# One layer of a conv / matrix-memory hybrid on eight cores: squares taken from the read-out itself, chunk steps and one merge projection in another order

## What is computed

```
proj = h @ w_in + b_in            # x, b, c (1024 each), q, k (512), v, o (1024), gates, gate_c, gate_m (1024)
y_conv = bg * causal_dwconv(cg * xin, conv_mix_w)
# matrix memory, per head (4 heads, dk 128, dv 256), in chunks of 128 rows
num = wts @ v + s_inter * (q @ C_prev);  den = rowsum(wts) + s_inter * (q @ n_prev)
h   = num / max(|den|, exp(-m_t))
C   = s_old * C + k_weighted^T @ v
hm  = sigmoid(o) * rmsnorm_per_head(h, g)      # h * rsqrt(mean(h*h) + EPS)
z   = sigmoid(gate_c) * (y_conv @ w_proj_conv) + sigmoid(gate_m) * (hm @ w_proj_mlstm)
x  += gt1 * (z @ w_out);  then a gated conv FFN, residual, final norm
```

## Time and profile before

| | us |
|---|---|
| median of 3 runs (1358.87 to 1362.21) | 1359.05 |
| the profiled execution, its own time | 1363.88 |
| its span, slowest core (core 2) | 1362.6 |
| spans of the eight cores | 1348.5 to 1362.6 |
| TensorE busy / VectorE / ScalarE | 1248.0 / 687.1 / 546.8 |
| mean granted TensorE clock, core 2 | 0.979 |

### The profile page before, as it was taken

How to read it: one execution, slowest core, us unless ns; L and a number is a source line. 1 busy time by engine, 2 the same in 40 slices (tenths; PEclk the granted TensorE clock), 3 DMA queues, 4 the chain that set the end, 5 groups by cost and what they waited for, 6 DMA issues and landing times.

```text
span 1362.6 us, 21331 instructions; the slowest of 8 cores (1348.5 to 1362.6 us)
## 1 busy us (share of the span) xinstructions
PE 1248.0 (92%) x7525; PEld 689.9 (51%) x7662; DVE 687.1 (50%) x1251; ACT 546.8 (40%) x1081; POOL 76.4 (6%) x149
## 2 busy tenths in 40 slices
PE   0588999998879999999989999988999999999997
PEld 0345455566656655666644444444544444444443
DVE  0473342586723356565654413467823365556534
ACT  2465113766522235554433331555521145544202
POOL 1000000000100000000000000000000000000000
PEclk9788999999989999999999999999999999999999
DMA  9968125388692465334264674313347074431603
GB/s 175 228 186 131 25 39 83 48 123 132 95 197 44 81 128 120 63 63 78 40 132 79 178 133 80 73 32 62 80 107 119 15 145 93 82 74 32 108 1 124
DMA packets 35128, 130.38 MB, mean 96 GB/s; under 512 B 2764, under 2 KB 3020, under 8 KB 35024
## 3 DMA queue, kind: packets, MB, share of 16 engines
q0 software_dynamic: 24944, 93.74, 41.1%
q1 hardware_dynamic: 10080, 35.27, 8.0%
HBM read 214.34 MB, written 8.39 MB: 163 GB/s over the span
## 4 chain that ended last, share of the span: by engine, by line
PE 83%; DMA 5%; DVE 5%; issue 3%; ACT 3%; POOL 0%; DVEq 0%; SPq 0%; ACTq 0%; POOLq 0%
PE psum L509 54%; PE psum L1270 11%; PE psum L805 4%; PE psum L1125 4%; DMA wslot<-w_in 3%; PE psum L1366 2%; PE psum L714 2%; PE psum L485 2%; DMA arena<-xin 1%; DMA arena<-bada_row 1%; PE psum L878 1%; ACT xnb L914 1%; DVE C L880 1%; ACT sqj L434 1%; ACT arena L871 1%
## 5 line engine op out<-in xcount | busy, mean ns | idle before, releaser
L509 PE MATMUL psum<-arena,wslot 128*128 128x512 bf16 (+1 forms) x4542 | 823.1, 338 | 17.1 <-DVE arena L926 9.0
L509 PEld LDWEIGHTS psum<-arena,wslot 128*128 128x128 bf16 x4640 | 452.6, 98 | 362.1 <-issue 24.0
L1199 DVE SCALAR_TENSOR_TENSOR arena<-arena,pcol_t 128x1028 f32<-128x1028 f32 (+1 forms) x88 | 113.2, 1287 | 92.8 <-ACT arena L1196 88.2
L1270 PE MATMUL psum<-wslot,arena 128*128 128x512 bf16 x688 | 151.8, 379 | 2.6 <-ACT arena L489 1.5
L1081 ACT ACTIVATE arena<-psum,pcol_t 128x512 bf16<-128x512 f32 (+1 forms) x80 | 47.9, 603 | 163.2 <-PE psum L509 162.2
L1270 PEld LDWEIGHTS psum<-wslot,arena 128*128 128x128 bf16 x704 | 68.9, 98 | 84.0 <-issue 2.0
L434 ACT ACTIVATE sqj<-arena 128x1024 bf16<-128x1024 f32 (+1 forms) x49 | 51.7, 1055 | 143.1 <-DVE arena L1273 97.4
L1201 ACT ACTIVATE arena<-arena 128x1028 f32<-128x1028 f32 (+1 forms) x44 | 46.6, 1059 | 121.1 <-DVE arena L1199 121.0
L1085 DVE TENSOR_TENSOR arena<-psum,arena 128x512 f32<-128x512 f32 (+1 forms) x40 | 23.4, 586 | 74.7 <-PE psum L509 73.8
L1125 PE MATMUL psum<-wslot,arena 128*128 128x512 bf16 (+1 forms) x264 | 59.2, 379 | 0.8 <-ACT arena L489 0.4
L805 PE MATMUL psum<-wslot,arena 128*128 128x512 bf16 (+1 forms) x266 | 58.9, 379 | 0.4 <-issue 0.2
(11 more groups left out here) (176 smaller groups left out, 1065.5 us busy)
## 6 DMA issues: line engine op xcount, KB each, us to landing
wslot<-w_in POOLq DMA_DIRECT2D x32, 1024.0 KB, 12.3
arena<-xin SPq DMA_DIRECT2D x32, 512.0 KB, 14.9
wslot<-w_ada POOLq DMA_DIRECT2D x12, 1024.0 KB, 15.5
wslot<-w_up_a POOLq DMA_DIRECT2D x10, 1024.0 KB, 9.8
wslot<-w_up_g POOLq DMA_DIRECT2D x10, 1024.0 KB, 12.2
wslot<-w_down POOLq DMA_DIRECT2D x8, 1024.0 KB, 8.6
y<-arena SPq DMA_DIRECT2D x16, 512.0 KB, 2.7
xt<-xin SPq DMA_DIRECT2D x15, 512.0 KB, 5.7
```

The source lines that it names most:

```text
L509: S.op("pe", lambda e: e.matmul(psum[:, b, 0:n], lhsT=wv[:, k, wcol0:wcol0 + 128], rhs=src[:, k, t0:t0 + n], start=(k == 0), stop=(k == 7) ...
L1199: S.op("dve", lambda e: e.scalar_tensor_tensor(out=t3[:, T0:NT], in0=a_s[:, s_ + T0:s_ + NT], scalar=pcol[:, cw + s_:cw + s_ + 1], in1=t3[ ...
L1270: S.op("pe", lambda e: e.matmul(psum[:, b, :], lhsT=act_t[jj][:, t0:t0 + 128], rhs=wv[:, jj % 8, :], start=(jj == 0), stop=(jj == NFF - 1) ...
```

## The change

1. `at_sq` squares `Xs` as it is, no longer scaled by `d4`, so it no longer waits for `at_den`. `at_den` ends with `d4*d4` in place of the reciprocal. A new step `at_rms` adds `256*EPS*d4^2` to the sum of squares on VectorE and takes the root on ScalarE. `at_f` is one reciprocal, its multiply is gone. (num/den/sqrt(mean((num/den)^2)+EPS) is num/sqrt(mean(num^2)+EPS*den^2).)
2. The table `parts` has other positions.
3. In the merge the memory projection of column block 0 is issued behind gate_c and conv of column block 1, and gate_m of block 1 behind it; from block 2 on the order is as before. No load moves on SP's queue; POOL issues the same weight loads in the same order.

```diff
-                S.op("dve", lambda e: e.reciprocal(out=d4[j][0:p], in_=d4[j][0:p]), reads=[r_d4[j]], writes=[r_d4[j]])
+                S.op("dve", lambda e: e.tensor_tensor(out=d4[j][0:p], in0=d4[j][0:p], in1=d4[j][0:p], op=ALU.mult), ...)
...
-                                                       scale=d4[j][0:p, h:h + 1], accum_out=s4[j][0:p, h:h + 1]),
-                         reads=[r_Xs[0], r_d4[j]], writes=[r_sqj, r_s4[j]])
-                if 3 in hh:
-                    S.op("act", lambda e: e.activation(out=s4[j][0:p], in_=s4[j][0:p], func=AF.Sqrt, scale=1.0 / 256, bias=EPS), ...)
+                                                       accum_out=s4[j][0:p, h:h + 1]),
+                         reads=[r_Xs[0]], writes=[r_sqj, r_s4[j]])
+            def at_rms(c):
+                S.op("dve", lambda e: e.scalar_tensor_tensor(out=s4[j][0:p], in0=d4[j][0:p], scalar=256.0 * EPS, in1=s4[j][0:p], op0=ALU.mult, op1=ALU.add), ...)
+                S.op("act", lambda e: e.activation(out=s4[j][0:p], in_=s4[j][0:p], func=AF.Sqrt, scale=1.0 / 256), ...)
...
-                S.op("dve", lambda e: e.tensor_tensor(out=f4[j][0:p], in0=f4[j][0:p], in1=d4[j][0:p], op=ALU.mult), ...)
...
-            parts = [(-0.42, at_K), (-0.52, at_A), (0.05, at_X), (0.22, lambda c: at_new(c, lo)), (0.22, at_den), (0.3, lambda c: at_new(c, hi)),
-                     (0.35, lambda c: at_sq(c, lo)), (0.45, lambda c: at_sq(c, hi)), (0.6, at_f), (0.7, lambda c: at_hm(c, lo)), (0.8, lambda c: at_hm(c, hi)),
-                     (1.45, lambda c: at_D(c, (0,))), (1.53, lambda c: at_D(c, (1,)))]
+            parts = [(-0.38, at_A), (-0.32, at_K), (0.05, at_X), (0.1, lambda c: at_sq(c, lo)), (0.15, at_den), (0.2, lambda c: at_sq(c, hi)),
+                     (0.27, lambda c: at_new(c, lo)), (0.35, lambda c: at_new(c, hi)), (0.4, at_rms), (0.5, at_f),
+                     (0.6, lambda c: at_hm(c, lo)), (0.7, lambda c: at_hm(c, hi)), (1.45, lambda c: at_D(c, (0,))), (1.53, lambda c: at_D(c, (1,)))]
...
-            todo += [... at_old(c, hh) ... for f, hh in ((0.4, lo), (0.5, hi))]
+            todo += [... at_old(c, hh) ... for f, hh in ((0.42, lo), (0.5, hi))]
...
+            for fn, j in [(merge_conv, 0), (merge_gate, 0), (merge_conv, 1), (merge_mem, 0), (merge_gate, 1), (merge_mem, 1)]:
+                fn(j)
+            for j in range(2, 8):
+                merge_conv(j)
+                merge_gate(j)
+                merge_mem(j)
```

More of the change, by code:

```diff
@@ L1072, in run_stage, with merge_ev_g, f, merge_conv @@
             ask_res(0, 6)
-            for j in range(8):
+            mt = {}
+            def merge_ev_g(j, col):
+                def f(b, t0, n):
+                    S.op("act", lambda e: e.activation(out=sg_t[j % 2][:, t0:t0 + n], in_=psum[:, b, 0:n], func=AF.Sigmoid,
+                                                       bias=pcol[:, PC_B + col + j:PC_B + col + j + 1]),
+                         reads=[r_bank[b], r_pc], writes=[r_sg[j % 2]])
+                return f
+            def merge_conv(j):
                 sg, zc, r_s, r_c = sg_t[j % 2], zc_t[j % 2], r_sg[j % 2], r_zc[j % 2]
                 if j % 4 == 0:
[L1076 to L1080, removed]
-                    S.op("act", lambda e: e.activation(out=sg[:, t0:t0 + n], in_=psum[:, b, 0:n], func=AF.Sigmoid, bias=pcol[:, PC_B + col:PC_B + col + 1]),
-                         reads=[r_bank[b], r_pc], writes=[r_s])
+                    for nm, src, o in (("gc", "in", IN_GC), ("pc", "pc", 0), ("gm", "in", IN_GM), ("pm", "pm", 0)):
+                        mt[nm] = load_w(src, o + (j // 4) * T)
                 def ev_pc(b, t0, n):
@@ L1106, in run_stage, with merge_mem, ev_pm @@
                                                           op=ALU.mult), reads=[r_wslot[si_w[i]], r_gt1], writes=[r_wslot[si_w[i]]])
-                proj(si_pm, wc, sgoT, lambda k, t0, n: [r_hm[c] for c in hit(chunks, t0, n)], tbs, ev_pm)
-                if j % 4 == 3:
-                    free_w(si_gm, si_pm)
+            def merge_mem(j):
+                sg, zc, r_s, r_c = sg_t[j % 2], zc_t[j % 2], r_sg[j % 2], r_zc[j % 2]
+                def ev_pm(b, t0, n):
+                    S.op("dve", lambda e: e.tensor_tensor(out=sg[:, t0:t0 + n], in0=psum[:, b, 0:n], in1=sg[:, t0:t0 + n], op=ALU.mult),
+                         reads=[r_bank[b], r_s], writes=[r_s])
+                    S.op("dve", lambda e: e.tensor_tensor(out=zT[:, j, t0:t0 + n], in0=sg[:, t0:t0 + n], in1=zc[:, t0:t0 + n], op=ALU.add),
+                         reads=[r_s, r_c], writes=[r_z[j][tbi(t0, n)[0]]])
+                proj(mt["pm"], (j % 4) * 128, sgoT, lambda k, t0, n: [r_hm[c] for c in hit(chunks, t0, n)], tbs, ev_pm)
+                if j % 4 == 3:
+                    free_w(mt["gm"], mt["pm"])
+            for fn, j in [(merge_conv, 0), (merge_gate, 0), (merge_conv, 1), (merge_mem, 0), (merge_gate, 1), (merge_mem, 1)]:
[4 more added lines that the diff above has]
+                merge_mem(j)
             r_h2 = new_h("h2", groups)
```

24 lines of the change are left out of this document (12 added, 12 removed).

## The result

| | before | changed |
|---|---|---|
| median (5 runs of each; 1358.87 to 1362.21, 1351.13 to 1353.83) | 1359.78 us | 1352.54 us |
| ratio, with its 95% interval | | 0.9944 [0.9932, 0.9955] |
| span of the slowest core, profiled execution | 1362.6 us | 1351.2 us |
| a core's waits of TensorE in the two chunk loops, without the one behind the first loop | 21.2 us | 15.6 us |

What follows compares the result with a forecast made beforehand. TensorE was taken as the bound, losing time to work queued behind VectorE's conv; second loop -4.6 and first loop +0.4 gave -4.2 us, so 1354.8 us from the median 1359.05, range 1350 to 1361.

Steps and rivals of the forecast that it cites:

- A1: Second stage, chunk 1's scores: TensorE waits 3.6 us for the state update behind the conv, plus 1.3 for the clock.
- +0.4 us: First chunk loop: waits and slow matmuls go from 11.2 to 11.8 us, +0.6 as walked, taken as 0.4 worse.
- D4: First stage, chunk 4's transposes: 3.2 us wait for chunk 5's first N behind the conv, plus 0.9.
- The edits' work: Both loops: 17 chunks by some 0.02 us of VectorE work is nothing; what counts is squares not waiting and step positions.
- beside A1's stall: Root's table load, 1.28 us, now behind a VectorE wait once per stage: between 0 and 1.3 us, taken as 0.
- The merge: Merge behind each chunk loop: new order costs nothing, since the first memory block did not wait for the last transposes.
- The new waits are smaller than walked: Rival, both loops: half of the 22 us of new waits may fall away, -9 us, 1350; chance 0.15.
- The shorter waits are dear too: Rival: two or three new waits of 1.4 to 2.3 us drop the clock, +1.3 each, about 1358; chance 0.2.
- one clean case at 1.93: Evidence against dear shorter waits: behind a TensorE wait of 1.93 us the next steps ran at their usual 0.94.
- The fixed price: TensorE's clock: 1.3 us more for each wait of about 3 us or more, nothing for shorter ones.
- Slower, keys behind the scaling: Rival, chunks with f behind the conv: key evacuations late, 3.4 us at four places, sum +9.4, 1368; chance 0.08.
- Nothing moves: Rival: the waits only change places, in the second loop as in the first, 1359 us; chance 0.12.

Runs made afterwards that it cites:

- the algebra alone: Kernel before with the new squares, denominator and root, at the step positions of before and with the merge of before: 1.0033 of before, 4.5 us slower.
- root early: Kernel before with the new algebra and old positions, but squares and root right behind each chunk's second N: 1.0002 of before.
- state update moved without and with the root: Changed kernel, second stage chunk 0: second N (heads 2 and 3) ahead of the last c block, 0.9969 of before; root step moved too, 0.9913.
- the order only: Changed kernel's positions and merge with the algebra of before, denominator just ahead of the squares: 0.9951 of before, 6.7 us faster.

## Why the prediction was right, point by point

**Where the time is won.** As forecast, in the second loop: 5.4 us, with 4.6 predicted. The waits for the copy fell from 11.0 to 0.6 us (2 or less predicted). A1 waited 3.48 (3.6), X4 1.82 (2.3), X2 0.99 and 0.37 (1.1 and 0.6), X3 0.52 (0.95), and X5 and X6 none; X1 had no wait where 0.6 was expected. What stands behind VectorE's lump of 4.6 us, minus what TensorE has to do meanwhile, gave each of these to within 0.6 us.

**The term that was mis-sized** is the first loop, "+0.4 us". It was 2.2 us of gain on core 2 (and 3.0 from X0 to X8 between the medians of the eight cores). These 2.6 us and the 0.8 of the second loop are what the forecast was short by: 4.2 forecast, 7.6 in the two loops by the traces, 7.2 by the medians. The big waits were right (D4 3.17 for 3.2, X2 1.90 for 2.1), the small ones too large: X1 0.30 for 1.4, D3 1.01 for 1.4, N7 0.59 for 0.95, X7 0.59 and 0.18 for 0.95, D7 0.29 for 0.4. Together they are 8.3 us, and 1.4 for the slow matmuls at D4, against 11.8 predicted with 0.9 for those at D4. The reason at X1 is in the trace of the changed kernel, core 2:

```profile
261.14 1.09 ACT L843 ACTIVATE arena<-psum,gm_wG 128x128 bf16<-128x128 f32 x4
...
261.47 0.27 PE L867 MATMUL psum<-arena 128*128 128x257 bf16 x1
...
262.37 0.27 PE L867 MATMUL psum<-arena 128*128 128x257 bf16 x1 [0.30 <-ACT arena L843]
```

Only the bank of head 2 waits for the keys; the read-outs of heads 0 and 1 run first, and the four evacuations of the keys had begun 0.33 us ahead of them. The prediction let the whole read-out wait. For the other small waits no experiment was made. That the forecast's total came out near is partly luck as well: the slow matmuls behind D4 cost 0, 1.3 or 2.8 us from X5 to X6 by core, and the kernel's time is that of the slowest core.

**The edits' work** was called nothing, in time rightly, but two things in that paragraph were missing. The squares became shorter, 0.40 us each for 0.49, 68 times: 6 of the 8.1 us that ScalarE lost. And the algebra's new link, VectorE's L906 ahead of ScalarE's root, was looked at only at the places the change gives it. It costs 4.5 us behind the conv (the algebra alone, by the ratios), nothing ahead of it (root early), and 5.7 us of the second loop once A1 no longer covers it (state update moved without and with the root: 12.7 and 18.2 us from X0 to X2, against 10.9 and 14.3). That the squares no longer wait for the denominator gave nothing by itself (1.0002 with the root early), and in the new order the 2.5 us by which the order only falls short, 2.2 of them in the second loop. The prediction had the table load "beside A1's stall" at 0, and that is what happened, the root 1.29 us behind the load's start:

```profile
874.16 1.28 ACT L908 ACT_TABLE_LOAD   x1 [6.19 <-DVE sml L906]
875.45 0.21 ACT L908 ACTIVATE sml<-sml 128x4 f32<-128x4 f32 x1
```

The 2.66 us of the Trainium skill ("ScalarE: Activation LUTs", "What ACT_TABLE_LOAD costs") did not show: neither here nor at any of the 16 table loads in each of three traces (before, changed, algebra only) was the next activation more than 1.30 us behind.

**The merge** was costed at nothing, and its order put back changed nothing (0.9932 against 0.9933).

**The rivals.** *The new waits are smaller than walked* came about in the first loop only. *The shorter waits are dear too*: not in the changed kernel, where 1.90 and 1.82 us left the clock alone on all eight cores. But it was nearer than its chance of 0.2 says: with the algebra of before the same wait was 2.06 us and cost 1.6 us more. And the "one clean case at 1.93" is not clean. It was read from 32 matmuls of one column (0.94 us), which take 0.95 us on core 5 of the same execution too, and there the next 8 matmuls take 3.34 us for 1.89:

```profile
344.54 0.38 PE L878 MATMUL psum<-arena 128*128 128x257 bf16 x2 [1.93 <-ACT arena L871]
...
345.96 3.34 PE L509 MATMUL psum<-arena,wslot 128*128 128x512 bf16 x8
```

The seven other cores lose nothing behind that wait. The fixed price, 1.3 us behind 3 us and nothing behind less, held at A1 (16 matmuls in 4.68 to 4.97 us for 3.62 on the eight cores), but not at D4. *Slower, keys behind the scaling*: the place was right, but X1 and X2 waited 0.3 to 0.4 us there, where the rival needed 2.1. It did come once the cover of A1 was taken away (2.02 us for L843 at X1). *Nothing moves* fell with the second loop.

**The median.** The forecast carried the profiled execution's sum over to the median as it stood, with the wait behind the first loop unchanged on each core. That wait was 9.0 us on one core of one execution before, and 2.8 to 4.8 after; its line is untouched by the change, and the 11.4 us between the two spans contain it. Medians of several runs, not these two spans, give the change's worth.

## What to carry to other kernels

Where one engine does a long lump (here 4.6 us of VectorE against 8-matmul blocks of 1.73), write down for every other engine what stands behind the lump in the queues, through all the links: VectorE's small step, ScalarE's root and table load, its evacuations, TensorE's bank. A step must be moved ahead of the lump together with the next one that depends on it; one link alone uncovered another wait and lost. And when an edit makes an engine wait where it did not, even for an operation of 0.15 us, price the wait by the queue it stands in, at each position the step could take.
